# Seventeen pairs of weight fetches of the first block move from GpSimd's DMA queue to SyncE's, behind the weight loads there

## The reference

```python
def retention_layer(x, w_in, w_out, pos):
    h = x @ w_in                              # 1024 -> 6144: q, k, v, g
    ...                                       # rope, chunked retention with a running state, norm
    return (jax.nn.silu(g) * r) @ w_out       # 2048 -> 1024
def swa_layer(x, w_in, w_out, sinks, k_band, v_band, bias, key_valid):
    h = x @ w_in                              # 1024 -> 2048: q, gate
    ...
    return (o * jax.nn.silu(gate)) @ w_out    # 1024 -> 1024
```

## Time and profile before

| | before |
|---|---|
| median of 3 runs | 2335.87 us (2333.92 to 2336.95) |
| the profiled execution | 2340.16 us |
| its span, first to last instruction | 2337.9 us |
| TensorE busy | 2290.1 us, 98% of the span |
| VectorE, ScalarE, GpSimd busy | 75%, 50%, 15% |
| granted TensorE clock, mean | 0.994 |
| fetches of raw sets, all 28 sets | 56 DMAs of 512 KB on GpSimd's queue |

### The profile page before, as it was taken

One profiled execution on the slowest core, in us unless ns is written; L12 is line 12 of the kernel. 1 busy time (PEld: TensorE's weight loads), 2 busy tenths in 40 slices (PEclk: granted clock), 3 DMA queues, 4 the chain that ended last, 5 costly groups with the idle time before them and its releaser, 6 DMA issues.

```text
span 2337.9 us, 30729 instructions
## 1 busy us (share of the span) xinstructions
PE 2290.1 (98%) x11554; PEld 1901.4 (81%) x11554; DVE 1756.7 (75%) x2439; ACT 1158.8 (50%) x1701; POOL 345.9 (15%) x346
## 2 busy tenths in 40 slices
PE   8999999999999999999999999999999999999997
PEld 6878877878888888887888888888888888888885
DVE  7888798875857669887596866897568667788548
ACT  4344455366435445636654544553655445554463
POOL 2311210222010110112201001110210110011132
PEclk9999999999999999999999999999999999999998
DMA  8787668653725435865484454585257345455323
GB/s 307 268 297 242 231 224 285 211 201 124 272 92 168 144 124 176 294 221 180 138 287 134 162 168 130 174 276 189 72 191 261 127 135 162 128 189 161 119 89 127
DMA packets 130899, 437.06 MB, mean 187 GB/s; under 512 B 13825, under 2 KB 18449, under 8 KB 130753
## 3 DMA queue, kind: packets, MB, share of 16 engines
q1 hardware_dynamic: 113088, 369.28, 47.7%
q0 software_dynamic: 17664, 65.83, 8.0%
HBM read 373.45 MB, written 57.41 MB: 184 GB/s over the span
## 4 chain that ended last, share of the span: by engine, by line
PE 83%; DVE 9%; DMA 4%; issue 3%; ACT 1%; SPq 0%; POOL 0%; DVEq 0%; ACTq 0%; POOLq 0%
PE accs L674 23%; PE accs L676 22%; PE accs L675 22%; PE bank L674 3%; PE bank L676 3%; PE bank L675 3%; DVE w_lo L1403 2%; PE bank L780 1%; PE bank L965 1%; PE bank L949 1%; PE bank L886 1%; PE bank L931 1%; DMA stage<-t_prep 1%; DMA stage<-w_qk 1%; PE accs L820 1%
## 5 line engine op out<-in xcount | busy, mean ns | idle before, releaser
L1403 DVE TENSOR_TENSOR w_lo<-stage,w_hi 128x1024 fp32r<-128x1024 f32 x524 | 643.8, 1236 | 330.0 <-ACT w_hi L1040 329.3
L1040 ACT ACTIVATE w_hi<-stage 128x1024 fp32r<-128x1024 f32 x524 | 550.3, 1055 | 482.6 <-PE accs L676 173.7
L674 PE MATMUL accs<-w_hi,xs 128*128 128x512 f32 x1136 | 450.5, 397 | 9.1 <-ACT sg L1045 6.4
L676 PE MATMUL accs<-w_hi,xs 128*128 128x512 f32 x1136 | 444.2, 391 | 0.0
L675 PE MATMUL accs<-w_lo,xs 128*128 128x512 f32 x1136 | 443.6, 390 | 0.0
L674 PEld LDWEIGHTS accs<-w_hi,xs 128*128 128x128 f32 x1136 | 213.9, 188 | 56.6 <-issue 12.1
L676 PEld LDWEIGHTS accs<-w_hi,xs 128*128 128x128 f32 x1136 | 213.8, 188 | 45.3
L675 PEld LDWEIGHTS accs<-w_lo,xs 128*128 128x128 f32 x1136 | 214.1, 188 | 42.3
L674 PE MATMUL accs<-x_hi,w_hi 128*128 128x512 f32 (+1 forms) x640 | 244.4, 382 | 1.9 <-DVE qT L1827 1.5
L2102 POOL TENSOR_TENSOR rstd<-ve,half 128x1 f32<-128x1 f32 x96 | 79.5, 829 | 1120.8 <-DVE ve L1473 880.3
L676 PE MATMUL accs<-x_hi,w_lo 128*128 128x512 f32 (+1 forms) x640 | 236.8, 370 | 0.0
(11 more groups left out here) (207 smaller groups left out, 3780.8 us busy)
## 6 DMA issues: line engine op xcount, KB each, us to landing
stage<-t_prep SPq DMA_DIRECT2D x208, 512.0 KB, 3.7
stage<-w_vg SPq DMA_DIRECT2D x100, 512.0 KB, 3.5
stage<-w_qk SPq DMA_DIRECT2D x64, 512.0 KB, 3.5
stage<-w_swa SPq DMA_DIRECT2D x64, 512.0 KB, 3.9
t_prep<-t_buf POOLq DMA_DIRECT2D x28, 1024.0 KB, 5.7
stage<-w_ro SPq DMA_DIRECT2D x48, 512.0 KB, 3.5
cs<-rope_t SPq DMA_DIRECT2D x16, 1024.0 KB, 7.8
t_buf<-w_vg POOLq DMA_DIRECT2D x32, 512.0 KB, 9.4
```

The source lines that it names most:

```text
L674: mm(dst, lhs[0], rhs[0], start=start, stop=False, skip_group_check=reopened)
L676: return mm(dst, lhs[1], rhs[0], start=False, stop=stop, skip_group_check=reopened)
L1040: copy(w_hi[:, RING[g] % HS], stage[:, RING[g] % LS], ACT.Copy).then_inc(w_hi_made, 1)
L1403: nc.vector.tensor_tensor(w_lo[:, RING[g] % LS], stage[:, RING[g] % LS], w_hi[:, RING[g] % HS].bitcast(F32), sub).then_inc(w_split, 1)
```

## The change

The 17 sets that are fetched in slots 1 to 69 of block 0 are now fetched by SyncE. At a slot with such a fetch SyncE first issues the weight load of that slot, then waits for what GpSimd waited for (the end of the slot before and, where the buffer was in use, the landing of its store), and issues the two DMAs. They signal semaphores of their own (`t_fetched`), for which VectorE waits at `begin_t`. GpSimd keeps the fetches of sets 4, 5 and 6, the eight late ones, and all stores.

```diff
+T_FETCHED = {n for n, _, _, load, _, _ in T_PLAN if 0 < load < RO}
...
+            def load_raw_set(n, at_slot):
+
+                b = T_BUF[n]
+                sp.wait_ge(products, used(at_slot - 1))
+                if T_NTH[n] > 1:
+                    sp.wait_ge(t_stored[b], 16 * (T_NTH[n] - 1))
+                for u in range(2):
+                    sp.dma_start(t_buf[b][:, u], raw_set(n)[:, u]).then_inc(t_fetched[b], 16)
...
                     load_pair(ahead(s * NP + p, LOAD_AHEAD))
+                    for n, _, in_block, at_slot, _, _ in T_PLAN:
+                        if (in_block, at_slot) == (s, p) and 0 < at_slot < RO:
+                            load_raw_set(n, at_slot)
...
-                dve.wait_ge(t_loaded[T_BUF[n]], 32 * T_NTH[n])
+                dve.wait_ge((t_fetched if n in T_FETCHED else t_loaded)[T_BUF[n]], 32 * T_NTH_LOAD[n])
...
             def load_t(n, in_block, at_slot):
...
-                if 0 < at_slot < RO:
-                    pool.wait_ge(products, used(at_slot - 1))
...
-                        if (in_block, at_slot) == (s, p):
+                        if (in_block, at_slot) == (s, p) and at_slot > RO:
                             load_t(n, in_block, at_slot)
```

More of the change, by code:

```diff
@@ L187 @@
 T_NTH = {n: [x[1] for x in T_PLAN[:T_RANK[n]]].count(b) for n, b, _, _, _, _ in T_PLAN}
+T_FETCHED = {n for n, _, _, load, _, _ in T_PLAN if 0 < load < RO}
+T_NTH_LOAD = {n: sum(m in T_FETCHED for m, c, _, _, _, _ in T_PLAN[:T_RANK[n]] if c == b) if n in T_FETCHED else
+              sum(m not in T_FETCHED for m, c, _, _, _, _ in T_PLAN[:T_RANK[n]] if c == b) for n, b, _, _, _, _ in T_PLAN}
 T_LAST_EARLY = [n for n, buf, _, load, _, _ in T_PLAN if buf == 4 and load < RO][-1]
@@ L366, in build @@
         t_loaded = [signal(f"t_loaded{i}") for i in range(5)]
+        t_fetched = [signal(f"t_fetched{i}") for i in range(5)]
         t_stored = [signal(f"t_stored{i}") for i in range(5)]
```

## The result

| | before | after |
|---|---|---|
| median | 2336.3 us (2333.92 to 2336.95, 4 runs) | 2353.1 us (2351.91 to 2354.06, 4 runs) |
| ratio | | 1.0068, 95% interval 1.0055 to 1.0081 |
| the profiled execution | 2340.16 us | 2354.06 us |
| its span | 2337.9 us | 2352.3 us |

The changed kernel is 16.8 us slower. The forecast was +7.9 us and 2343.8; the range ended at 2349.0, so the time lies outside it. The direction is right, and the forecast is about half of what was measured.

What follows compares the result with a forecast made beforehand. It took TensorE, busy 2290.1 of 2337.9 us, as the bound. Start 5.2, clock 1.7 and 118 to 158 us 1.0 gave +7.9 us on the median 2335.9, so 2343.8 us, range 2334 to 2349.

Steps and rivals of the forecast that it cites:

- What bounds it: Whole kernel: TensorE, busy 2290.1 of 2337.9 us; 24 us saved on GpSimd are worth nothing by themselves.
- issue cost: Seventeen DMA pairs moved to SyncE at 0.33 us per DMA: taken as 0, from -0.5 to +0.5 us.
- The start: 17 to 40 us: slot 6's weight pair lands at 36.7 behind set 7; TensorE idles 5.2 us before slot 4.
- The clock's share: After the idle time at the start: TensorE's clock falls, and 1.7 us of work are lost.
- if they go at the same pace: At the start: set 7's two DMAs take 3.2 us each in SyncE's queue, like a weight load, giving 36.7 us.
- The signs that were named: Slot 6's pair lands at 35 us or later, `qrT` starts after 36, TensorE waits 4 to 6 us before slot 4.
- 118 to 158 us: Middle of block 0: 1 to 5 us idle at slot 27, mostly repaid at 149; +1.0 us, from -5.8 to +6.
- the middle stretch is not repaid: Rival: slot 27's pair 6.4 us late, TensorE idles 4.7 there, the wait at 149 stays; +13.3, 2349 us, chance 0.14.
- faster: Rival: weight loads land earlier from 118 us, slot 33's pair 4 us or more before 146.2; -5.6, 2330.3 us, chance 0.10.
- No change: Rival: slot 6's pair lands at 32.9, TensorE loses 1.4 us without a clock fall, rest zero; 2337 us, chance 0.24.

Runs made afterwards that it cites:

- e5: The changed kernel with sets 7, 8, 14 and 15 given back to GpSimd, the bias store again waiting behind them; 2338.42 us, ratio 1.0006 to the kernel before.
- e4: The changed kernel with GpSimd holding the bias store until TensorE has finished slot 24; 2346.9 us, ratio 1.0041 to the kernel before.
- e7: The changed kernel with sets 7 and 8 fetched in slots 4 and 5 and the bias store issued after slot 44; 2342.4 us, ratio 1.0025 to before.
- e1: The changed kernel with only sets 7 and 8 fetched by SyncE, the other fifteen by GpSimd as before; 2343.07 us, ratio 1.0027 to the kernel before.
- e6: The changed kernel with sets 7 and 8 fetched in slots 4 and 5 instead of 1 and 2; 2342.06 us, ratio 1.0019 to the kernel before.
- e8: The kernel before, all fetches on GpSimd, with the bias store issued when TensorE has finished slot 44; 2340.76 us, ratio 1.0011 to before.
- e9: The kernel before, all fetches on GpSimd, with the bias store issued when TensorE has finished slot 32; 2336.11 us, ratio 1.0001 to before.
- e10: The kernel before, all fetches on GpSimd, with the bias store issued when TensorE has finished slot 55; 2338.7 us, ratio 1.0005 to before.
- e2: The changed kernel with only sets 14 and 15 fetched by SyncE, the bias store early as in the changed kernel; 2339.66 us, ratio 1.0016 to before.
- e11: The changed kernel with sets 7 and 8 fetched in slots 4 and 5 and the bias store at slot 56; 2340.83 us, ratio 1.0017 to before.
- e3: The changed kernel with all fetches back on GpSimd and the bias store early, ahead of the fetch of set 14; 2338.39 us, ratio 1.0007 to before.

## Why the prediction was half right

**What bounds it, and issue cost: right.** 25 us less on GpSimd bought nothing, and e5 shows thirteen moved fetches without a cost that can be told from zero. One thing was off in detail: DMAs on SyncE took longer to issue than the 0.33 us that I read in the earlier trace rows (1.58 us for the pair of slot 27), and set 14's fetch waited until 127.79 for a store. The next weight load was issued 0.9 us late by it, not 0.3, and in e4 and e7 by 1.8 and 2.2: a small part of the middle's loss is this term.

**The start: right, a little low.** The pair of slot 6 was to land at 36.7 and landed at 37.4; the idle time was to be 5.2 us and was 5.8; with the clock 6.9 was forecast and 8.4 measured (39.71 to 48.14). The clock's share is therefore 2.6 us, not 1.7. By slot 21, 6.6 were left: two small waits of the kernel before (0.76 us at 57.5, 0.68 at 72.1) were no longer met. e1 and e6 put it on sets 7 and 8 alone. The sentence "if they go at the same pace" held to 0.7 us. The signs that were named came: landing after 35, the copy at 38.40, a wait of 5.8.

"Issuing engines are not separate DMA queues" in "DMA: Bandwidth & Descriptors" of the Trainium skill says that transfers share the 16 engines whoever starts them, and that starting them from several engines only saves issuing time. Of the bytes the traces agree: from 24 to 36 us 4.72 MB were moved, where it was 4.78. Of the time they do not: who issues also decides what a transfer stands behind, and that, with the bias store's new place behind the stores of sums, was worth 0.68% here.

**118 to 158 us: the step that failed.** The text said: "None of these bytes vanishes, and all of them were moved before the pair of slot 33 landed ... TensorE at 153.6", so that the middle repays what slot 27 loses, apart from 1.0 us. Measured from slot 21 to 37: +6.7, where +1.0 was forecast. The bytes were there, but they are not alike. I counted the bias store as 0.75 MB at the common rate, 2 us at the earlier trace rows's 398 GB/s; it took 3.7 us of all 16 engines already before, and 6.2 in its new place. Set into that hole and behind the 1 MB of set 14 (set 15 is issued behind it), the pair of slot 27 took 8.2 us longer than before from its issue and landed 9.1 later against TensorE's own place, where I had allowed 6.4 at most. TensorE idled 7.5 us, not 1 to 5, and paid 2.6 for the clock, which I had not charged there (10.1 from slot 21 to 28). The repayment did come, as foreseen: 5.8 us from slot 28 to 33, which is the old wait of 4.05 and its 1.7 of clock. Then 2.4 more were lost up to slot 37, with waits of 1.15 us for `v_lo` and 0.4 for `sg`.

The information was there to be read. The kernel before has such a hole too, a shorter one (before: DMA view, 138 to 144 us, in 40 slices):

```profile
DMA  9999999998999959876985959989999998898889
GB/s 382 393 447 413 321 270 321 263 208 174 150 174 174 150 140 181 143 137 133 229 195 184 280 215 307 382 338 348 355 389 359 352 321 321 328 294 328 300 273 300
```

For 2 us after 139 the engines are busy for the most part and move 130 to 230 GB/s. The wait of 4.05 us is what comes of it: e8, e9 and e10 each remove it by moving this one store. I had put that wait down to full queues.

**The rival "the middle stretch is not repaid"** had the mechanism (the pair of slot 27 late, TensorE waiting at slot 27 with a fall of the clock) and the nearest number, +13.3. Its claim that the wait at 149 stays was wrong, and that slot 37 also stands at +13.3 is luck: 6.9 were counted for the start and 6.6 left at slot 21; the middle lost 10.1 where 6.4 were counted, was repaid 5.8 where nothing was, and then lost 2.4 more. The rival "faster" fell at its condition: the pair of slot 33 landed at 158.8, not 4 us before 146.2. "No change" fell with the start, where the pair of slot 6 landed at 37.4, not 32.9.

**The parts don't add up.** At slot 37, e1 and e2 together are 7.1 us late and the changed kernel 13.3. Of the 6.2 between them 2.4 are what e1 gets back after slot 21 and the changed kernel doesn't, since its middle has a worse wait than the one that e1 shortened; 2.2 are a middle that loses more there than in e2 (6.7 against 4.5); the other 1.6 stand already at slot 21 and are differences between single executions in part. Why the middle is 2.2 us worse than in e2, I can't say; in e6, where the start isn't late, it loses 5.6, so the late start can be at most half of it.

**Open.** What makes a packet of the bias store take 0.33 to 0.74 us was not tried: it reads the same 768-byte rows of 16 partitions again and again (64 copies of each), and a store in larger rows, from more partitions or in pieces would tell. Nor is it known why the DMAs behind a fetch take SyncE up to 3.2 us to issue. And what lies between slot 68 and the medians (3.7 us in the changed kernel, 6.9 in e11) can't be told from chance with one profile a kernel; runs of one kernel lay up to 14 us apart.

## What to carry to other kernels

A prefetch that isn't urgent must not stand ahead of an urgent load in the same first-in first-out queue: look, for each load that a busy engine waits for, at what was issued just ahead of it, and follow the engine's own order behind it (here the copy of q stood behind the late pair's high part). Don't count DMAs by bytes alone: find each one's rate while it is under way, and where the DMA share is full but the GB/s are low, name the transfer that does it, since moving it may only move the hole (waits came with it in e3 and in e7 to e10). When a removed instruction also held back what stood behind it in its queue, that follower's new place is part of the change.

## What the runs showed of the hardware

- The bias store (768 KB, 1024 rows of 768 bytes from 16 partitions) moved at about 100 GB/s with a DMA share of 1.0 in e9: 0.74 us a packet of 4.6 or 3 KB over the whole store, where the packets of that queue take 0.15 in the earlier trace rows. In the kernel before it took 0.33 a packet, with SyncE's queue moving beside it (1.07 MB from 138 to 144 us). While it was under way in e9, SyncE's queue moved nothing that the view from 160 to 167 us lists; its two loads issued there, at 162.2 and 164.9, took 10.8 and 9.3 us.
- The same raw fetch goes in smaller packets from SyncE's queue: from 24 to 36 us in the changed kernel (DMA view)

```profile
q0 software_dynamic: 717, 2.61, 56.4%
q1 hardware_dynamic: 902, 2.10, 46.4%
```

  that is 2.3 KB a packet on SyncE's queue and 3.6 on GpSimd's. In the packet records, SyncE's are 656 of 2 KB (the fetches) and 184 of 4 KB (as its weight loads before). Per megabyte both queues' packets take 2.6 us of 16 engines (0.464 x 12 / 2.10 and 0.564 x 12 / 2.61), so the smaller packets cost nothing here. With more to move, SyncE's queue got 2.10 MB in these 12 us, after 1.35 before. "Queues, rings and completion order" in "DMA: Bandwidth & Descriptors" of the Trainium skill has the engines take turns between queues packet by packet; the counts of packets, 717 to 902 here and 931 to 375 before, are not equal shares, though no view says how much of these times both queues had work. In e9 SyncE's two loads had been issued, and all 170 packets up to 167 us are GpSimd's: there the trace shows no turns.
- Idle times of 5.8 and 7.5 us were each followed by 2.6 us of loss at the lower of the two clock levels, 1.2 instead of 2.4 GHz (a granted clock of 0.72 from 40 to 50 us, 0.56 from 140 to 150); in e2, 7.8 us of idle time by 2.0. After the 2.61 us in e1 the clock didn't fall (1.00 from 150 to 160 us), and after the 1.57 and 2.07 us in e3, 5.8 us apart, it did (0.83 from 135 to 145).
